# The low part of the down weights: made by Pool at the head of a turn, in place of VectorE

## The chip, the core and the metric

The kernel runs on one core of one Trainium2 chip. The metric is the time of one execution on the device in microseconds, taken as the median of several runs. TensorE (PE) multiplies matrices, VectorE (DVE), ScalarE (ACT) and Pool (GpSimd) work on tiles element by element, and SyncE (SP) issues the loads and stores.

## What is computed

One step of a two-layer decoder over 1024 prompt tokens and 8 x 8 sample tokens: layer 0 mixes tokens by latent attention, layer 1 by causal pooling, and each is followed by a gated FFN with a short causal convolution. The part that matters here is that FFN (from the reference):

```python
D_MODEL, D_FF, CONV_W = 1024, 2816, 3

def conv_ffn(h, prev, w_up, conv_w, conv_b, w_down):
    T = h.shape[1]
    u = h @ w_up
    up = jnp.concatenate([prev.astype(u.dtype), u], axis=1)
    conv = conv_b + up[:, 0:T] * conv_w[0]
    for k in range(1, CONV_W):
        conv = conv + up[:, k:k + T] * conv_w[k]
    y = (jax.nn.silu(conv[..., :D_FF]) * conv[..., D_FF:]) @ w_down
    return y, up[:, -CONV_BUF:]
```

## The kernel before

All is float32, kept with model or FFN rows on the partitions and tokens along the columns. TensorE multiplies in a shorter format, so each operand is split into a high part (ACT copies it into fp32r) and a low part (the difference), and a product is three matmuls: high x high, high x low, low x high.

The change lies in the last stage, `tail_stage`, whose FFN runs in 88 **turns** n = 0 to 87 (the code calls them pairs): two layers, in each the tokens in two halves, 22 turns to each of the four stretches. A **first half** (turns 0 to 21 and 44 to 65) has 512 columns, worked in one piece; a **second half** (turns 22 to 43 and 66 to 87) has 576, in two pieces of 288. Turn n covers 128 gate rows and the 128 up rows that go with them, and uses three weight tiles of 128 x 1024:

- G and U, the gate and the up weights of turn n. TensorE makes G, then U (`up`, lines 2742 to 2744), in 8 steps a piece.
- D, down weights. They lag: between the up steps of turn n, at places that tables fix (`DOWN_AT`), TensorE makes the down products of turn n-2 (`down`, lines 2706 to 2708), with g = silu(gate) x up of the two turns 2j and 2j+1. A D tile covers half of the model rows for both of these turns. So the first down product of an even turn n waits for g of turn n-1, and that of an odd turn finds it made.

Each tile goes the same way: SP loads it into one of two `raw` buffers, ACT makes `w_hi` (`split_hi`, L2380), and VectorE makes `w_lo` (`split_lo`, L2511), counted by the semaphore `lo_ready`. Loading, high and low parts all follow one list, `order`: U of turn n, G of turn n+1, D of turn n-1, and so on. A `raw` buffer is loaded again when the low part of its tile is done. There is one D slot: its high part waits for the last down product of the tile before, which stands near the end of a turn, so ACT makes D's high part at the very end of a turn and VectorE its low part at the head of the next.

What VectorE does in the head of turn n, in this order: D of n-2 (L2511), in a first half U of n too (L2511 again), the convolution of U of turn n-1 (L2530, L2535 for the samples), g = gate x up (L2542), then, when ACT has copied g into `g_hi` (L2435), its low part `g_lo` (L2548). Later in the turn come additions of the down products out of PSUM into `y` (L2563), the convolution of G, and the low part of the next G; in a second half U's too.

Beside it run `Chain`s, the norms and mixers of the other half of the tokens, cut into six ticks a turn that every engine goes through in program order. On Pool a chain has additions of squares (L2102), additions to the residual x (L2107), and in the pooling mixer of layer 1 window sums (L2061, L2151). Turns of a chain's quiet parts and the last 15 turns have nothing on Pool.

Every engine runs its own instructions in program order and waits at semaphores. The order within each is written out by hand.

Of the kernel before, what the change touches and what calls it, by code (L numbers as in the profile page):

```python
# [18 lines left out]
ALU = mybir.AluOpType  # L19
# [89 lines left out]
class Kernel:  # L109
# [22 lines left out]
    def sem(self, name):  # L132

        self.sems.append(self.nc.alloc_semaphore(name=name))
        return self.sems[-1]
# [1346 lines left out]
N_PAIRS = 4 * PAIRS  # L1482
SLOTS = 6
TICKS = SLOTS * PAIRS
# [4 lines left out]
G, U, D = range(3)  # L1489
# [87 lines left out]
class Tail:  # L1577


    def __init__(self, k, own):  # L1580
# [23 lines left out]
        sem = lambda name: k.sem("t_" + name)  # L1604
# [4 lines left out]
        self.hi_ready = sem("hi_ready")  # L1609
        self.lo_ready = sem("lo_ready")  # L1610
        self.o_hi_ready, self.o_lo_ready = sem("o_hi_ready"), sem("o_lo_ready")
# [572 lines left out]
def tail_stage(k):  # L2184
    nc, io = k.nc, k.io
    with ExitStack() as own:
        t = Tail(k, own)
# [3 lines left out]
        chains = []  # L2191
# [9 lines left out]
        order = [("out", j) for j in range(OUT_UNITS)] + [(G, 0)]  # L2201
# [3 lines left out]
        number = {what: o for o, what in enumerate(order)}  # L2205

        def slot(s, n):

            if s == "out":
                return (n + 1) % 3  # L2210
            return G if s == D and n == N_PAIRS - 2 else s

        def unit(s, n):
# [3 lines left out]
            return io["ffn_w"][n // PAIRS // 2, n % PAIRS, s]  # L2217

        def conv_steps(s, n):

            whole, rest = divmod(n, PAIRS)
            each = (2, 4) if s == G else (2, 6)
            return sum(each[q % 2] for q in range(whole)) * PAIRS + each[whole % 2] * rest
# [43 lines left out]
        def _(sp):  # L2267
            def load(o):
                if o >= 2:
                    sp.wait_ge(t.lo_ready, o - 1)  # L2270
                sp.dma_start(t.raw[o % 2][:], unit(*order[o])).then_inc(t.raw_in[o % 2], 16)
# [69 lines left out]
            sp.wait_ge(t.x_out, 80)  # L2341

        @block.gpsimd
        def _(pool):
            pool.memset(t.y[0][:, :, 0:BUF], 0.0).then_inc(t.zeroed, 1)
            for j in range(OUT_UNITS):
                chains[0].pool(pool, 2 * j)
                chains[0].pool(pool, 2 * j + 1)
            pool.wait_ge(t.x_in[1], 16)
            for chain in chains[1:5]:  # L2350
                for tick in range(TICKS):
                    chain.pool(pool, tick)
            for tick in range(SLOTS):
                chains[5].pool(pool, tick)
# [151 lines left out]
        def split_lo(dve, s, n):  # L2506

            o = number[s, n]
            dve.wait_ge(t.hi_ready, o + 1)
            i = slot(s, n)  # L2510
            dve.tensor_tensor(t.w_lo[i][:], t.raw[o % 2][:], t.w_hi[i][:], ALU.subtract).then_inc(t.lo_ready, 1)  # L2511
# [54 lines left out]
        def _(dve):  # L2566
# [21 lines left out]
            for n in range(N_PAIRS):  # L2588
                q, p = divmod(n, PAIRS)
# [7 lines left out]

                if n >= 2:
                    split_lo(dve, D, n - 2)
                if not half_of(n):  # L2600
# [35 lines left out]
                else:  # L2636
# [19 lines left out]
                    sums(*((3, 4) if few else (7, 8)))  # L2656
            split_lo(dve, D, N_PAIRS - 2)
            split_lo(dve, D, N_PAIRS - 1)
            convolve(dve, U, N_PAIRS - 1, 1)
# [8 lines left out]
        def _(pe):  # L2668
            def out_unit(j, c):
                half = j // KT  # L2670
                cols, bank = piece(half, c), out_bank(j, c)
                pe.wait_ge(t.lo_ready, number["out", j] + 1)
                if j >= KT + 2:
# [15 lines left out]
            def down(r):  # L2689
# [4 lines left out]
                bank = down_bank(r)[:, 0:cols.stop - cols.start]  # L2694
                pe.wait_ge(t.lo_ready, number[D, m] + 1)
                pe.wait_ge(t.g_lo_ready, before(first + 1) + c + 1)
# [26 lines left out]
            def up(s, n, c):  # L2723
# [5 lines left out]
                places = DOWN_AT[half][len(downs) > 4]  # L2729
                pe.wait_ge(t.lo_ready, number[s, n] + 1)  # L2730
                bank_free(s, n, c)
# [213 lines left out]
```

## Time and profile before

| | us |
|---|---|
| median of 3 runs (2517.59 to 2523.27) | 2517.89 |
| the profiled execution | 2525.76 |
| its span, first to last instruction | 2522.9 |
| PE busy in it | 2405.1 |
| DVE busy in it | 1678.1 |
| ACT busy in it | 1229.2 |
| POOL busy in it | 340.2 |

The profile is of one execution. Its times are in microseconds from the first instruction; busy times do not count waits at semaphores. A row of a timeline says when an instruction started, how long it took, its engine, line and tiles, and in brackets how long the engine had been idle before it and what released it. "x2" merges two neighbours that follow each other; their time is then that from the start of the first to the end of the last. An instruction's time includes what it stands and waits for inside the engine.

### The profile page before, as it was taken

How to read it: one execution, taken by the hardware profiler on the slowest of the kernel's cores; microseconds unless marked ns; L12 is line 12 of the kernel's file. 1: busy time of each engine (PE TensorE's matmuls, PEld its weight loads, DVE VectorE, ACT ScalarE, POOL GpSimd, SP SyncE). 2: the span in 40 equal slices, each digit the busy share in tenths (PEclk: the TensorE clock that was granted, in tenths of full speed). 3: DMA queues.
4: the chain of work that ended last, by engine and by line, in shares of the span. 5: the costliest groups of instructions: out<-in, count | busy, mean ns of one | idle time of the engine just before them, and what ended most of it. 6: DMA issues, size and time to landing. Idle time of an engine off the chain costs nothing.

```text
span 2522.9 us, 40509 instructions
## 1 busy us (share of the span) xinstructions
PE 2405.1 (95%) x15148; PEld 2059.6 (82%) x15148; DVE 1678.1 (67%) x2953; ACT 1229.2 (49%) x2734; POOL 340.2 (13%) x365
## 2 busy tenths in 40 slices
PE   7989999998989989999999999999999999999996
PEld 6966666766668878888899999997778889999995
DVE  5655666666234678666677858777866877766666
ACT  4444444443234655434556455555645555444443
POOL 0000000000004240000131113013222202100003
PEclk9999999999899999999999999999999999999998
DMA  7022223225534223232322222232223222232221
GB/s 274 13 93 93 97 93 116 101 102 210 191 111 163 76 76 96 89 100 92 109 84 76 76 71 81 77 116 97 91 70 100 91 93 82 93 110 78 89 80 69
DMA packets 71714, 253.50 MB, mean 100 GB/s; under 512 B 7874, under 2 KB 15426, under 8 KB 64610
## 3 DMA queue, kind: packets, MB, share of 16 engines
q1 hardware_dynamic: 71090, 250.78, 29.2%
q8 instruction: 122, 2.00, 0.3%
q14 instruction: 70, 0.57, 0.1%
q10 hardware_dynamic: 432, 0.15, 0.0%
HBM read 243.83 MB, written 7.07 MB: 99 GB/s over the span
## 4 chain that ended last, share of the span: by engine, by line
PE 61%; DVE 6%; issue 1%; ACT 1%; POOL 1%; DMA 0%; DVEq 0%; POOLq 0%; ACTq 0%
PE psum L2743 12%; PE psum L2744 12%; PE psum L2742 12%; PE psum L2706 6%; PE psum L2707 6%; PE psum L2708 6%; DVE t_conv L2530 1%; PE psum L2684 1%; PE psum L2686 1%; PE psum L2685 1%; DVE t_w_lo L2511 1%; PE psum L2178 1%; DVE t_y L2563 1%; PE psum L2163 1%; POOL t_stat L2102 1%
## 5 line engine op out<-in xcount | busy, mean ns | idle before, releaser
L2742 PE MATMUL psum<-t_h,t_w_hi 128*128 128x288 f32 (+1 forms) x2112 | 699.2, 331 | 3.4 <-DVE t_w_lo L2511 3.4
L2743 PE MATMUL psum<-t_h,t_w_hi 128*128 128x288 f32 (+1 forms) x2112 | 693.5, 328 | 0.0
L2744 PE MATMUL psum<-t_h,t_w_lo 128*128 128x288 f32 (+1 forms) x2112 | 692.8, 328 | 0.0
L2742 PEld LDWEIGHTS psum<-t_h,t_w_hi 128*128 128x128 f32 x2112 | 397.5, 188 | 36.9 <-DVE t_w_lo L2511 5.4
L2743 PEld LDWEIGHTS psum<-t_h,t_w_hi 128*128 128x128 f32 x2112 | 397.6, 188 | 31.5
L2744 PEld LDWEIGHTS psum<-t_h,t_w_lo 128*128 128x128 f32 x2112 | 398.0, 188 | 27.9
L2563 DVE TENSOR_TENSOR t_y<-psum,t_y 128x288 f32<-128x288 f32 (+1 forms) x480 | 255.1, 532 | 247.7 <-PE psum L2708 245.7
L2511 DVE TENSOR_TENSOR t_w_lo<-t_raw,t_w_hi 128x1024 fp32r<-128x1024 f32 x280 | 350.9, 1265 | 83.3 <-ACT t_w_hi L2380 83.1
L2380 ACT ACTIVATE t_w_hi<-t_raw 128x1024 fp32r<-128x1024 f32 x280 | 295.6, 1066 | 175.0 <-PE psum L2708 157.4
L2706 PE MATMUL psum<-t_g_hi,t_w_hi 128*128 128x288 f32 (+1 forms) x1056 | 348.4, 330 | 16.3 <-issue 7.2
L2530 DVE SCALAR_TENSOR_TENSOR t_conv<-t_u,t_taps,t_conv 128x512 f32<-128x512 f32 (+2 forms) x440 | 307.4, 699 | 80.1 <-ACT t_conv L2418 75.3
L2707 PE MATMUL psum<-t_g_lo,t_w_hi 128*128 128x288 f32 (+1 forms) x1056 | 346.7, 328 | 0.0
L2708 PE MATMUL psum<-t_g_hi,t_w_lo 128*128 128x288 f32 (+1 forms) x1056 | 346.4, 328 | 0.0
L2102 POOL TENSOR_TENSOR t_stat<-t_stat,t_sq 128x256 f32<-128x256 f32 (+1 forms) x196 | 185.3, 949 | 1148.8 <-ACT t_sq L1882 1141.8
L2706 PEld LDWEIGHTS psum<-t_g_hi,t_w_hi 128*128 128x128 f32 x1056 | 198.5, 188 | 37.6 <-issue 16.5
L2707 PEld LDWEIGHTS psum<-t_g_lo,t_w_hi 128*128 128x128 f32 x1056 | 198.4, 188 | 15.6
L2708 PEld LDWEIGHTS psum<-t_g_hi,t_w_lo 128*128 128x128 f32 x1056 | 198.6, 188 | 15.1
L2409 ACT ACTIVATE t_u<-psum 128x512 f32<-128x512 f32 (+2 forms) x264 | 116.8, 442 | 133.0 <-PE psum L2744 116.5
L2435 ACT ACTIVATE t_g_hi<-t_conv 128x288 fp32r<-128x288 f32 (+1 forms) x132 | 66.8, 506 | 229.7 <-DVE t_conv L2542 229.5
L2418 ACT ACTIVATE t_conv<-psum,t_taps 128x288 f32<-128x288 f32 (+1 forms) x264 | 174.3, 660 | 0.0
L1141 PE MATMUL psum<-keys,q 128*128 128x512 f32 (+3 forms) x384 | 150.8, 502 | 3.4 <-ACT prob L921 2.2
L928 ACT ACTIVATE prob_t<-psum 128x512 f32<-128x512 f32 (+3 forms) x128 | 66.1, 517 | 139.9 <-PE psum L1157 137.4
(215 smaller groups left out, 3375.3 us busy)
## 6 DMA issues: line engine op xcount, KB each, us to landing
t_raw<-in_ffn_w SPq DMA_DIRECT2D x264, 512.0 KB, 3.5
late_w<-in_ada_late SPq DMA_DIRECT2D x40, 1024.0 KB, 4.8
cache<-in_cache SPq DMA_DIRECT2D x64, 320.0 KB, 4.7
t_raw<-in_wo SPq DMA_DIRECT2D x16, 512.0 KB, 3.3
ada_w<-in_ada_w SPq DMA_DIRECT2D x6, 1024.0 KB, 8.5
proj_raw<-in_proj_w SPq DMA_DIRECT2D x8, 448.0 KB, 7.9
x<-in_pair_w SPq DMA_DIRECT2D x4, 768.0 KB, 5.3
x<-in_x SPq DMA_DIRECT2D x1, 2304.0 KB, 11.7
```

The source lines that it names most:

```text
L2102: pool.tensor_tensor(acc, acc, t.sq[:, r % 2, 0:self.T], ALU.add).then_inc(t.added, 1)
L2380: act.activation(t.w_hi[slot(s, n)][:], t.raw[o % 2][:], ACT.Copy).then_inc(t.hi_ready, 1)
L2418: act.activation(t.conv[s][:, cols], bank[:, 0:n_all], ACT.Identity, bias=t.taps[:, layer, m, 3:4], scale=t.taps[:, layer, m, 2:3]).then_i ...
L2511: dve.tensor_tensor(t.w_lo[i][:], t.raw[o % 2][:], t.w_hi[i][:], ALU.subtract).then_inc(t.lo_ready, 1)
L2530: dve.scalar_tensor_tensor(prompt, u[:, tap + first:tap + last], by, prompt, ALU.mult, ALU.add)\
L2563: dve.tensor_tensor(y, out, y, ALU.add).then_inc(t.acc_done, 1)
L2706: pe.matmul(bank, t.w_hi[i][:, o], hi, start=e == 0, stop=False)
L2707: pe.matmul(bank, t.w_hi[i][:, o], lo, start=False, stop=False)
L2708: last = pe.matmul(bank, t.w_lo[i][:, o], hi, start=False, stop=e == 1)
L2742: pe.matmul(bank, t.w_hi[s][:, o], hi, start=kt == 0, stop=False)
L2743: pe.matmul(bank, t.w_hi[s][:, o], lo, start=False, stop=False)
L2744: last = pe.matmul(bank, t.w_lo[s][:, o], hi, start=False, stop=kt == KT - 1)
```

## The change

Two methods are new. `split_down_lo` lets Pool wait for the high part of D of turn n, subtract, and count a semaphore of its own, `down_lo_ready`. `low_part` lets an engine wait for the low part of a tile: for D by that semaphore, for the others by `lo_ready`, renumbered without the D tiles. SP (before it loads a `raw` buffer again) and TensorE (`up`, `down` and the output projection) wait through it. Pool makes D of n-2 at the head of its ticks of turn n, from turn 2 on, and the last two D tiles after the last turn. The three calls on VectorE go.

```diff
-        self.lo_ready = sem("lo_ready")
+        self.lo_ready, self.down_lo_ready = sem("lo_ready"), sem("down_lo_ready")
...
+        lo_number = {what: sum(w[0] != D for w in order[:o]) for o, what in enumerate(order)}
+
+        def low_part(eng, s, n):
+
+            if s == D:
+                eng.wait_ge(t.down_lo_ready, n + 1)
+            else:
+                eng.wait_ge(t.lo_ready, lo_number[s, n] + 1)
...
-                    sp.wait_ge(t.lo_ready, o - 1)
+                    low_part(sp, *order[o - 2])
...
+        def split_down_lo(pool, n):
+
+            o = number[D, n]
+            pool.wait_ge(t.hi_ready, o + 1)
+            i = slot(D, n)
+            pool.tensor_tensor(t.w_lo[i][:], t.raw[o % 2][:], t.w_hi[i][:], ALU.subtract).then_inc(t.down_lo_ready, 1)
...
-            for chain in chains[1:5]:
+            for q, chain in enumerate(chains[1:5]):
                 for tick in range(TICKS):
+                    n, at = divmod(TICKS * q + tick, SLOTS)
+                    if at == 0 and n >= 2:
+                        split_down_lo(pool, n - 2)
                     chain.pool(pool, tick)
+            split_down_lo(pool, N_PAIRS - 2)
+            split_down_lo(pool, N_PAIRS - 1)
...
-                if n >= 2:
-                    split_lo(dve, D, n - 2)
                 if not half_of(n):
                     split_lo(dve, U, n)
...
-            split_lo(dve, D, N_PAIRS - 2)
-            split_lo(dve, D, N_PAIRS - 1)
...
-                pe.wait_ge(t.lo_ready, number[D, m] + 1)
+                low_part(pe, D, m)
```

The line numbers of the last stage are some 20 higher after the change: L2511 becomes L2532, L2530 L2551, L2542 L2563, L2548 L2569, L2563 L2584; Pool's split is L2357.

On VectorE, the head of turn 6 (a first half) before: the two splits at its start are D of turn 4 and U of turn 6, the convolution is that of U of turn 5.

```order
L2563 TENSOR_TENSOR t_y<-psum,t_y 128x512 x2
L2511 TENSOR_TENSOR t_w_lo<-t_raw,t_w_hi 128x1024 x2
L2530 SCALAR_TENSOR_TENSOR t_conv<-t_u,t_taps,t_conv 128x512 x2
L2542 TENSOR_TENSOR t_conv<-t_conv 128x512
L2548 TENSOR_TENSOR t_g_lo<-t_conv,t_g_hi 128x512
L1943 SCALAR_TENSOR_TENSOR t_scaled<-x,ada,t_stat 128x288
```

The same place after:

```order
L2584 TENSOR_TENSOR t_y<-psum,t_y 128x512 x2
L2532 TENSOR_TENSOR t_w_lo<-t_raw,t_w_hi 128x1024
L2551 SCALAR_TENSOR_TENSOR t_conv<-t_u,t_taps,t_conv 128x512 x2
L2563 TENSOR_TENSOR t_conv<-t_conv 128x512
L2569 TENSOR_TENSOR t_g_lo<-t_conv,t_g_hi 128x512
L1943 SCALAR_TENSOR_TENSOR t_scaled<-x,ada,t_stat 128x288
```

One of the two splits is gone; U's is now the first of the head, and all behind it is as it was.

On Pool, turns 25 and 26 before, where a chain squares and adds:

```order
L2107 TENSOR_TENSOR x<-x,t_y 128x256 x3
L2102 TENSOR_TENSOR t_stat<-t_stat,t_sq 128x256
L2107 TENSOR_TENSOR x<-x,t_y 128x256
L2102 TENSOR_TENSOR t_stat<-t_stat,t_sq 128x256
L2107 TENSOR_TENSOR x<-x,t_y 128x256
L2102 TENSOR_TENSOR t_stat<-t_stat,t_sq 128x256
L2107 TENSOR_TENSOR x<-x,t_y 128x256
L2102 TENSOR_TENSOR t_stat<-t_stat,t_sq 128x256 x2
```

And after:

```order
L2107 TENSOR_TENSOR x<-x,t_y 128x256 x2
L2102 TENSOR_TENSOR t_stat<-t_stat,t_sq 128x256
L2107 TENSOR_TENSOR x<-x,t_y 128x256
L2102 TENSOR_TENSOR t_stat<-t_stat,t_sq 128x256
L2107 TENSOR_TENSOR x<-x,t_y 128x256
L2102 TENSOR_TENSOR t_stat<-t_stat,t_sq 128x256
L2107 TENSOR_TENSOR x<-x,t_y 128x256
L2357 TENSOR_TENSOR t_w_lo<-t_raw,t_w_hi 128x1024
L2102 TENSOR_TENSOR t_stat<-t_stat,t_sq 128x256 x2
```

The split of turn 26 stands behind the last x addition of turn 25 and ahead of the additions of turn 26; that of turn 25 stands between the first and the second of the three x additions.

## Rows read from the trace of the kernel before

**Rows 1.** The page, part 1: busy time, share of the span, instructions.
```profile
PE 2405.1 (95%) x15148; PEld 2059.6 (82%) x15148; DVE 1678.1 (67%) x2953; ACT 1229.2 (49%) x2734; POOL 340.2 (13%) x365
```
**Rows 2.** TensorE's waits in the whole span: total us, times, longest.
```profile
PE psum L2163 <- POOL t_stat L2102: 13.3, 4, 5.4
PE psum L2706 <- issue: 7.2, 7, 1.4
...
PE psum L2706 <- DVE t_w_lo L2511: 5.6, 6, 1.6
...
PE psum L2742 <- DVE t_w_lo L2511: 3.4, 4, 1.6
PE psum L2706 <- DVE t_y L2563: 3.0, 5, 1.3
```
**Rows 3.** Groups by shape: busy us, mean ns of one, idle before it.
```profile
L2511 DVE TENSOR_TENSOR t_w_lo<-t_raw,t_w_hi 128x1024 fp32r<-128x1024 f32 x280 | 350.9, 1265 | 83.3 <-ACT t_w_hi L2380 83.1
...
L2102 POOL TENSOR_TENSOR t_stat<-t_stat,t_sq 128x288 f32<-128x288 f32 x98 | 93.3, 955 | 587.6 <-ACT t_sq L1882 583.8
...
L2061 POOL TENSOR_TENSOR t_rooms<-t_y 128x1052 f32<-128x1052 f32 x4 | 8.2, 2055 | 83.4 <-ACT t_y L1902 55.9 <-DVE t_y L2038 27.6
```
**Rows 4.** Timelines of turn 52; then line 2563: min/median/max ns, first and last start.
```profile
1803.04 2.13 POOL L2061 TENSOR_TENSOR t_rooms<-t_y 128x1052 f32<-128x1052 f32 x1 [26.10 <-ACT t_y L1902]
1803.89 2.37 DVE L2511 TENSOR_TENSOR t_w_lo<-t_raw,t_w_hi 128x1024 fp32r<-128x1024 f32 x1
...
L2563 DVE TENSOR_TENSOR t_y<-psum,t_y x480: 441/458/694, 927.5 to 2500.6; 128x288 f32<-128x288 f32 x106, 128x512 f32<-128x512 f32 x54
```
**Rows 5.** Timelines of ACT, DVE and PE in the head of turn 6.
```profile
952.45 2.01 ACT L2380 ACTIVATE t_w_hi<-t_raw 128x1024 fp32r<-128x1024 f32 x2 [5.08 <-PE psum L2708]
...
954.89 0.78 ACT L2418 ACTIVATE t_conv<-psum,t_taps 128x512 f32<-128x512 f32 x1
...
953.54 2.36 DVE L2511 TENSOR_TENSOR t_w_lo<-t_raw,t_w_hi 128x1024 fp32r<-128x1024 f32 x2 [0.46 <-ACT t_w_hi L2380]
955.82 1.53 DVE L2530 SCALAR_TENSOR_TENSOR t_conv<-t_u,t_taps,t_conv 128x512 f32<-128x512 f32 x2
...
958.78 0.69 DVE L2548 TENSOR_TENSOR t_g_lo<-t_conv,t_g_hi 128x512 fp32r<-128x512 f32 x1 [0.70 <-ACT t_g_hi L2435]
...
959.75 0.39 PE L2706 MATMUL psum<-t_g_hi,t_w_hi 128*128 128x512 f32 x1
```
**Rows 6.** The same two steps, DVE and PE, in the head of turn 64.
```profile
2036.20 0.69 DVE L2548 TENSOR_TENSOR t_g_lo<-t_conv,t_g_hi 128x512 fp32r<-128x512 f32 x1 [0.70 <-ACT t_g_hi L2435]
...
2037.17 0.39 PE L2706 MATMUL psum<-t_g_hi,t_w_hi 128*128 128x512 f32 x1
```
**Rows 7.** The same two steps in the head of turn 50.
```profile
1775.59 0.69 DVE L2548 TENSOR_TENSOR t_g_lo<-t_conv,t_g_hi 128x512 fp32r<-128x512 f32 x1 [0.70 <-ACT t_g_hi L2435]
...
1776.39 0.47 PE L2706 MATMUL psum<-t_g_hi,t_w_hi 128*128 128x512 f32 x1 [1.32 <-issue]
```
**Rows 8.** Timelines of DVE and PE in the head of turn 78, a second half.
```profile
2293.50 1.23 DVE L2511 TENSOR_TENSOR t_w_lo<-t_raw,t_w_hi 128x1024 fp32r<-128x1024 f32 x1 [0.69 <-ACT t_w_hi L2380]
...
2296.52 0.30 PE L2706 MATMUL psum<-t_g_hi,t_w_hi 128*128 128x288 f32 x1
```
**Rows 9.** Timelines of DVE, POOL and PE in the head of turn 26, a second half.
```profile
1296.36 1.22 DVE L2511 TENSOR_TENSOR t_w_lo<-t_raw,t_w_hi 128x1024 fp32r<-128x1024 f32 x1
...
1296.52 1.55 POOL L2107 TENSOR_TENSOR x<-x,t_y 128x256 f32<-128x256 f32 x1 [2.62 <-DVE t_y L1991]
...
1298.48 0.30 PE L2706 MATMUL psum<-t_g_hi,t_w_hi 128*128 128x288 f32 x1
```
**Rows 10.** Timeline of PE at the first down product of turn 31.
```profile
1398.88 0.40 PE L2706 MATMUL psum<-t_g_hi,t_w_hi 128*128 128x288 f32 x1 [0.93 <-DVE t_w_lo L2511]
```

More of the change, by code:

```diff
@@ L2671, in out_unit @@
                 cols, bank = piece(half, c), out_bank(j, c)
-                pe.wait_ge(t.lo_ready, number["out", j] + 1)
+                low_part(pe, "out", j)
                 if j >= KT + 2:
@@ L2729, in up @@
                 places = DOWN_AT[half][len(downs) > 4]
-                pe.wait_ge(t.lo_ready, number[s, n] + 1)
+                low_part(pe, s, n)
                 bank_free(s, n, c)
```

## The prediction

> **What bounds the kernel now.** I read the page first, then who waited for whom on TensorE, then the timelines around the moved step, turn by turn. The page says that TensorE (PE) is busy for 95% of the span, VectorE (DVE) for 67%, Pool for 13% [rows 1]. So work taken off VectorE is worth only what TensorE waits for it. In the 88 FFN turns those waits are few [rows 2]: 7.2 us in 7 waits in front of the first down product of a turn (L2706) that the profile puts to "issue", 5.6 us in 6 for a low part of weights, 3.0 us in 5 for an accumulation, and 3.4 us in 4 in front of an up product. Together that is 19 us of 2523: the most that a lighter VectorE could give. The 13.3 us at L2163 are for Pool's own adds.
>
> The "issue" waits are explained by a timeline. In turn 50 VectorE's subtraction for the low part of g (L2548) ends at 1775.59 + 0.69 = 1776.28, and the waiting matmul starts at 1776.39, 0.1 us later [rows 7]: TensorE waits for g_lo. This holds in every even turn of a first half (512 columns), and in turns 22 and 66 behind them, because the down products of an even turn need the g of the turn just ended, and that g is finished only in the head of the same turn: VectorE makes the low part of the down weights (D), then that of the up weights (U), then the convolution of U (L2530), the product (L2542), ACT copies it, VectorE makes g_lo, and TensorE starts L2706. I count 18 such turns from turn 4 on: in ten of them g_lo ends 0.1 us ahead of the matmul (7 of these are the "issue" waits), in eight 0.28 us ahead. The eight are 6, 10, 12, 14, 16, 20, 58 and 64; the first and the last stand in [rows 5] and [rows 6]: 958.78 + 0.69 = 959.47 against 959.75, and 2036.89 against 2037.17. Since a matmul released by g_lo starts 0.1 us after it, the true slack in these is 0.18 us. **This chain, not VectorE's share of busy time, is what the change must be priced on.**
>
> **The moved step's price.** 88 subtractions of 128x1024 leave VectorE, where one takes 1.265 us in the mean [rows 3]; back to back they follow each other every 1.14 us (two and the start of the convolution: 955.82 - 953.54 = 2.28) [rows 5]. That is 88 x 1.14 = 100 us of VectorE, nearly all of it beside TensorE work. On Pool no row has this width with this output type. The nearest is the 128x1052 addition, 2055 ns; 2055 x 1024/1052 gives 2.00 us. The far end is the 128x288 addition's 955 ns, which by columns gives 3.40 us, though it has its fixed part and its blocked cases in it [rows 3]. I take 2.05 us, by the row nearest in size; 2.0 to 3.4 stay for the range. A start on Pool after ACT's signal I set at 0.08 us, an estimate.
>
> **What Pool does to VectorE.** In turn 52 a Pool addition ran from 1803.04 to 1805.17; VectorE's split, started inside it at 1803.89, took 2.37 us instead of 1.22 and ended 1.09 us after Pool [rows 4]. So VectorE did not share, it stood until Pool was through. The accumulations of L2563, which read PSUM and one SBUF tensor, never exceeded 694 ns in 480 cases, Pool or not [rows 4]: only VectorE's instructions with two SBUF inputs stand. It goes the other way too: in turn 26 Pool's 128x256 addition started at 1296.52, while VectorE's split ran, and took 1.55 us [rows 9]. The splits, convolutions, products and g_lo all have two SBUF inputs. The Trainium skill, in "SBUF — State Buffer", section "Who interferes with whom", speaks against this change: it calls the hold an exclusive lock for the whole instruction, with whichever of the two starts second stopped until the first is through. The trace agrees (2.37 against 1.22 us); without such a lock the sum would be rival 1 below.
>
> **Turn 6, step by step** [rows 5]. ACT's two copies take 2.01 us together; the first ends at 953.51, the second at 954.46. Before: D on VectorE at 953.54, U behind it, convolution at 955.82; ACT has had its input ready since 954.89 + 0.78 = 955.67. After: Pool starts D at 953.59 and ends at 955.64. VectorE's U is ready at 954.46, but stands until Pool ends; it ends 1.09 later and the convolution starts 0.08 ahead of that end, so at 956.64: 0.82 us later than before, although an instruction has left the queue. g_lo ends at 960.29, TensorE starts at 960.39 instead of 959.75: **0.64 us lost**. TensorE makes nothing of it good, since the next turn's head starts from its own last product.
>
> **The sum.**
> - Eight such turns x 0.64 = 5.1 us.
> - Turns 8, 18 and 62, whose slack is used up (0.1 us) without a visible wait: 0.4, 0.8, 0.8 = 2.0 us.
> - Turns 22 and 66: U comes later there, and the convolution waits for ACT until 1.2 us after D's high part. Pool holds it until 2.0: 0.7 each = 1.4 us.
> - Turns 4, 48, 50, 52 and 60 have the wait already, and Pool's additions ahead of the split; the convolution comes 0.85 to 1.3 us later: 5.0 us.
> - Turn 3: TensorE waits at L2163 for additions of Pool [rows 2], and the split now stands between them; 1.0 us, from 0.5 to 1.9.
> - Second halves, ordinary turns: the first down product starts 3.02 us after D's split may start (2296.52 - 2293.50) [rows 8]. Pool's needs 0.05 to start, 2.05, and 0.06 to reach TensorE. Nothing lost; the convolution comes 0.8 us later, covered by the time that is left before U's low part is wanted half a turn later.
> - Turns 26 to 28 and 37 to 39: one of Pool's x additions is still ahead of the split in its order. In turn 26 it starts at 1296.52; with about 0.74 us for itself the split starts at 1297.3 at the earliest and ends at 1299.3, but TensorE wants it at 1298.48 [rows 9]: 0.9 us, or 1.3 if a piece of the convolution gets in between. Four such turns at 1.0, two with 0.7 us more room at 0.25: 4.5 us.
> - Turns 30, 31 and 41 to 43, where TensorE waits for D itself. In turn 31 it has been idle since 1398.88 - 0.93 = 1397.95 [rows 10], and D, which released it, began 1.22 + 0.06 us before 1398.88, at 1397.60. Pool's ends at 1399.7: 0.8 us worse. The others, where VectorE was late itself: 0.3 to 0.4 each. 2.3 us.
> - The end of turn 87, where both splits of the last pair stand in Pool and the convolution behind them: 0.8 us.
> - Turns 53 and 54, where VectorE is full: D off its queue against Pool's holds, three times 1.1 against up to 2.0; I take 0, plus or minus 3.
>
> Sum 22.1 us. The loads lose nothing: SP's load of the next G waits for D, comes 0.8 us later, and lands some microseconds before ACT wants it. The added semaphore stops Pool until D's high part is there; behind it stand that turn's additions, and behind them ACT's squares (two buffers), in turns that hold no second chain mostly none.
>
> The profiled execution took 2525.76 us (span 2522.9), 7.9 above the median of 2517.89; a difference made on its trace is put on the median: 2517.9 + 22.1 = **2540 us**. With the terms' own spread (2.0 to 2.3 us for the split on some 27 places, minus 1 to plus 7; turn 3, turns 26 to 39 and turns 53, 54, about 5 either way) 2531 to 2550.
>
> Of Pool's price the Trainium skill's "GPSIMD Engine Reference", section "Performance versus the Vector engine", gives 4497 ns for 2048 columns; half is 2.25 us as an estimate. By that the sum would be 22.1 + 27 x 0.2 = 27.5 us, 2545. The trace's 1052 columns in 2.06 us speak for less.
>
> **Rivals.**
> 1. *Side by side.* Pool's split and VectorE's U run without stopping each other. Then U starts at ACT's second signal, the waits that hang on VectorE's queue go (7.2 of "issue" less 2.8 in turns 22 and 66, 3.4 and 3.0 [rows 2]: 10.8 us), and D comes 0.9 us later where TensorE waits for it (1.5 us): 9 us faster, 2509. It decides for faster as soon as the hold costs under 0.2 us. Against it: the 2.37 us of [rows 4]. Chance 8%.
> 2. *A slow Pool.* The fp32r output or the subtraction goes at the 955 ns row's rate, 3.4 us. Then every place above costs 1.35 more (36 us), and in the second halves D lands 3.5 us after the signal against 3.05: 0.5 us in some 34 turns. 22 + 36 + 17 = 75 us, 2593. For it: no row of Pool writes fp32r. Against it: on VectorE the type costs nothing, 1.22 us for 1024 columns. Chance 15%, anywhere from 2550 up.
> 3. *A draw.* The stops in the clean turns are real (8 us with turns 8, 18, 22, 62 and 66), but in the busy turns 4 and 48 to 60 VectorE gains 1.14 us a turn and Pool's hold falls onto accumulations that read PSUM and are not stopped; the gains there take back 5 of the 8: about 2521. For it: L2563 stands among the heads' steps. Chance 15%.
>
> The forecast has 62%. A measurement of this kernel can tell about 0.3% (7.6 us) from no change: slower is the forecast and rival 2, 77%; within it is rival 3 with a part of rival 1, 18%; faster 5%. The range 2517 to 2556 leaves out rival 1 and most of rival 2.
>
> **What will show it.** Pool's split at 1.9 to 2.3 us; VectorE's U beginning in first-half heads before Pool ends and lasting up to 2.2 us instead of 1.22; a wait of 0.5 to 0.8 us in front of L2706 in even turns of first halves, put to "issue" or to g_lo; L2706 waiting for Pool in turns 26 to 39; no new waits in turns 73 to 87. I am wrong if U is not stretched (rival 1), if Pool's split is over 2.9 us (rival 2), or if the waits appear and the total does not.

## The result and the profile after

The changed kernel took 2571.81 us, the median of 3 runs (2571.66 to 2573.66), against 2517.89: a ratio of 1.0212, 95% interval [1.0192, 1.0232]. In a later job (runs measured together), with four runs of it and seven of the kernel before, it was 2568.64 against 2522.78: 1.0186 [1.0166, 1.0205]. So the change costs 46 to 54 us. The direction was forecast, the size was not: 22 us were.

The page of the changed kernel, part 1, answers to [rows 1]:

```profile
PE 2417.4 (94%) x15148; PEld 2065.0 (80%) x15148; DVE 1688.6 (66%) x2865; ACT 1230.2 (48%) x2734; POOL 549.7 (21%) x453
```

VectorE has 88 instructions less and is busy 10 us longer. Where that comes from, the groups by shape show (busy us, mean ns of one; see [rows 3]):

```profile
L2532 DVE TENSOR_TENSOR t_w_lo<-t_raw,t_w_hi 128x1024 fp32r<-128x1024 f32 x192 | 283.6, 1478 | 106.4 <-ACT t_w_hi L2401 106.4
...
L2551 DVE SCALAR_TENSOR_TENSOR t_conv<-t_u,t_taps,t_conv 128x512 f32<-128x512 f32 x264 | 223.9, 848 | 67.0 <-ACT t_conv L2439 63.3
```
```profile
L2357 POOL TENSOR_TENSOR t_w_lo<-t_raw,t_w_hi 128x1024 fp32r<-128x1024 f32 x88 | 217.1, 2468 | 796.8 <-ACT t_w_hi L2401 796.6
```

The remaining splits on VectorE take 1478 ns in the mean instead of 1265: they stand. Pool's split takes 2468 ns, where the prediction took 2.05 us. TensorE's waits in the whole span (total us, times, longest), beside [rows 2]:

```profile
PE psum L2723 <- issue: 27.5, 20, 3.0
PE psum L2723 <- POOL t_w_lo L2357: 14.8, 12, 2.1
PE psum L2163 <- POOL t_stat L2102: 14.7, 5, 6.4
...
PE psum L2759 <- DVE t_w_lo L2532: 5.4, 4, 2.1
PE psum L2723 <- DVE t_y L2584: 5.4, 6, 1.8
```

L2723 is the first down product (L2706 before). Its waits put to "issue" (that is, to g_lo) grew from 7.2 us in 7 to 27.5 in 20, and those for D from 5.6 in 6 to 14.8 in 12.

**Turn 6**, against [rows 5], ACT, POOL, DVE, DVE, DVE and PE:

```profile
953.02 2.01 ACT L2401 ACTIVATE t_w_hi<-t_raw 128x1024 fp32r<-128x1024 f32 x2 [4.86 <-PE psum L2725]
...
954.16 2.41 POOL L2357 TENSOR_TENSOR t_w_lo<-t_raw,t_w_hi 128x1024 fp32r<-128x1024 f32 x1 [4.84 <-ACT t_w_hi L2401]
...
955.06 2.59 DVE L2532 TENSOR_TENSOR t_w_lo<-t_raw,t_w_hi 128x1024 fp32r<-128x1024 f32 x1 [1.41 <-ACT t_w_hi L2401]
957.57 1.53 DVE L2551 SCALAR_TENSOR_TENSOR t_conv<-t_u,t_taps,t_conv 128x512 f32<-128x512 f32 x2
...
960.52 0.69 DVE L2569 TENSOR_TENSOR t_g_lo<-t_conv,t_g_hi 128x512 fp32r<-128x512 f32 x1 [0.70 <-ACT t_g_hi L2456]
...
961.31 0.47 PE L2723 MATMUL psum<-t_g_hi,t_w_hi 128*128 128x512 f32 x1 [0.83 <-issue]
```

Pool's split starts 0.08 us after ACT's signal and ends at 956.57. VectorE's U starts 0.90 us into it, is shown with 2.59 us, and ends at 957.65, 1.08 after Pool: its own work begins when Pool is through. All behind it follows, and TensorE idles.

**Turn by turn.** The time from one turn's first up product to the next one's (for turn 87, to TensorE's last product), after minus before, sums to 50.4 us over the 88 turns. 35.4 us of it are longer waits of TensorE (one in front of a turn's first up product counts with the turn before), 15.0 us are products that run slower or start again behind a wait. Behind TensorE's last product the changed kernel gains 0.8 us, and ahead of turn 0, where nothing changed, its profile is 2.7 us shorter. By the terms of the prediction's sum:

| turns | forecast | turns longer by | of it TensorE's waits |
|---|---|---|---|
| 6, 10, 12, 14, 16, 20, 58, 64 | 5.1 | 9.2 | 7.1 |
| 8, 18, 62 | 2.0 | 3.6 | 3.2 |
| 22, 66 | 1.4 | 4.9 | 2.0 |
| 4, 48, 50, 52, 60 | 5.0 | 13.2 | 7.7 |
| 3 | 1.0 | 0.5 | 1.0 |
| 26 to 28, 37 to 39 | 4.5 | 7.7 | 6.2 |
| 30, 31, 41 to 43 | 2.3 | 5.3 | 5.0 |
| 53, 54 | 0 | 1.4 | 0.5 |
| turn 87 and behind it | 0.8 | 1.1 | 1.3 |
| 5, 45, 46, 55, 56, 61 | not named | 2.6 | 1.4 |
| all others | 0 | 0 | 0 |

Every place that was named lost, and hardly any other did. What was wrong is the size of nearly every term.

### The profile page after: what moved, and what is told of

It reads as the page before. It is cut to its first block, busy times and chain, and to the rows that moved or that the text cites. A ratio compares the mean times of both kernels' runs of the same rounds, so it can differ in the third digit from the quotient of the medians.

```text
span 2569.8 us, 40509 instructions
## 1 busy us (share of the span) xinstructions
PE 2417.4 (94%) x15148; PEld 2065.0 (80%) x15148; DVE 1688.6 (66%) x2865; ACT 1230.2 (48%) x2734; POOL 549.7 (21%) x453
## 4 chain that ended last, share of the span: by engine, by line
PE 54%; DVE 8%; issue 3%; ACT 3%; POOL 2%; DMA 1%; ACTq 0%; DVEq 0%; POOLq 0%
PE psum L2759 11%; PE psum L2760 11%; PE psum L2761 11%; PE psum L2723 6%; PE psum L2725 6%; PE psum L2724 6%; DVE t_conv L2551 3%; DVE t_w_lo L2532 2%; PE psum L2701 1%; PE psum L2703 1%; PE psum L2702 1%; PE psum L2178 1%; POOL t_stat L2102 1%; DVE t_y L2584 1%; ACT t_w_hi L2401 1%
## 5 line engine op out<-in xcount | busy, mean ns | idle before, releaser
L2551 DVE SCALAR_TENSOR_TENSOR t_conv<-t_u,t_taps,t_conv 128x512 f32<-128x512 f32 (+2 forms) x440 | 369.6, 840 | 143.2 <-ACT t_conv L2439 137.9
L2723 PE MATMUL psum<-t_g_hi,t_w_hi 128*128 128x288 f32 (+1 forms) x1056 | 352.2, 334 | 47.8 <-issue 27.5
L2584 DVE TENSOR_TENSOR t_y<-psum,t_y 128x288 f32<-128x288 f32 (+1 forms) x480 | 254.8, 532 | 209.5 <-PE psum L2725 208.3
L2357 POOL TENSOR_TENSOR t_w_lo<-t_raw,t_w_hi 128x1024 fp32r<-128x1024 f32 x88 | 217.1, 2468 | 796.8 <-ACT t_w_hi L2401 796.6
L2532 DVE TENSOR_TENSOR t_w_lo<-t_raw,t_w_hi 128x1024 fp32r<-128x1024 f32 x192 | 283.6, 1478 | 106.4 <-ACT t_w_hi L2401 106.4
L2725 PE MATMUL psum<-t_g_hi,t_w_lo 128*128 128x288 f32 (+1 forms) x1056 | 348.4, 330 | 0.0
L2723 PEld LDWEIGHTS psum<-t_g_hi,t_w_hi 128*128 128x128 f32 x1056 | 199.6, 189 | 74.3 <-issue 42.8
L2102 POOL TENSOR_TENSOR t_stat<-t_stat,t_sq 128x256 f32<-128x256 f32 (+1 forms) x196 | 189.9, 973 | 285.6 <-ACT t_sq L1882 278.5
L2725 PEld LDWEIGHTS psum<-t_g_hi,t_w_lo 128*128 128x128 f32 x1056 | 199.9, 189 | 15.7
```

What stands on the lines that cost most here:

```text
L2102: pool.tensor_tensor(acc, acc, t.sq[:, r % 2, 0:self.T], ALU.add).then_inc(t.added, 1)
L2357: pool.tensor_tensor(t.w_lo[i][:], t.raw[o % 2][:], t.w_hi[i][:], ALU.subtract).then_inc(t.down_lo_ready, 1)
L2551: dve.scalar_tensor_tensor(prompt, u[:, tap + first:tap + last], by, prompt, ALU.mult, ALU.add)\
L2584: dve.tensor_tensor(y, out, y, ALU.add).then_inc(t.acc_done, 1)
L2723: pe.matmul(bank, t.w_hi[i][:, o], hi, start=e == 0, stop=False)
L2725: last = pe.matmul(bank, t.w_lo[i][:, o], hi, start=False, stop=e == 1)
```

## Experiments

**1. Is it the bookkeeping?** VectorE makes D again, at the old place, on the new semaphore.

```diff
...
-                        split_down_lo(pool, n - 2)
...
+                if n >= 2:
+                    split_down_lo(dve, n - 2)
                 if not half_of(n):
                     split_lo(dve, U, n)
...
```

> The low part of D is made by VectorE again, at its old place, but counted on its own semaphore, and SyncE and TensorE wait through the new rule. Chain theory (Pool's split holds VectorE's head of a turn, or lands too late): nothing is left to cost, 2518 us, within 5 us of the kernel before. Rival, the bookkeeping (own semaphore, renumbered waits, the order in which SyncE sees the two raw buffers free): it carries a good part of the 54 us, 2530 to 2572 us.

Measured: 2521.39 us, ratio 0.9994 [0.9982, 1.0005]; the turns differ from those of the kernel before by 0.3 us in sum. The semaphore, the renumbered waits and SyncE's order cost nothing.

**2. Is it the length of Pool's split?** Half of its columns.

```diff
-            pool.tensor_tensor(t.w_lo[i][:], t.raw[o % 2][:], t.w_hi[i][:], ALU.subtract).then_inc(t.down_lo_ready, 1)
+            some = slice(0, D_MODEL // 2)
+            pool.tensor_tensor(t.w_lo[i][:, some], t.raw[o % 2][:, some], t.w_hi[i][:, some], ALU.subtract).then_inc(t.down_lo_ready, 1)
```

> Pool makes only the first 512 of the 1024 columns of D's low part; the low part of the other half is left out of the computation. Everything else is as in the changed kernel. Chain theory: the split takes about 1.27 us instead of 2.41, ends before VectorE's U would have been through, and the 0.83 us waits of the even first-half turns go altogether; what stays is a rest in turns 28, 39, 48 to 60: 2521 to 2530 us. Rival, price by duration: half of the 54 us stays, about 2545. Rival, the place (one more engine in the chain, whatever it does there): 2555 us or more.

Measured: 2521.71 us, ratio 0.9993 [0.9983, 1.0003]. Half the length takes away not half of the loss but all of it. Turn 6 of this run, POOL and DVE:

```profile
947.90 1.29 POOL L2358 TENSOR_TENSOR t_w_lo<-t_raw,t_w_hi 128x512 fp32r<-128x512 f32 x1 [4.84 <-ACT t_w_hi L2402]
```
```profile
948.81 1.48 DVE L2533 TENSOR_TENSOR t_w_lo<-t_raw,t_w_hi 128x1024 fp32r<-128x1024 f32 x1 [1.41 <-ACT t_w_hi L2402]
950.21 1.53 DVE L2552 SCALAR_TENSOR_TENSOR t_conv<-t_u,t_taps,t_conv 128x512 f32<-128x512 f32 x2
```

U stands for 0.4 us only, and the convolution starts 2.39 us after D's high part (947.82) against 2.31 before: the 0.18 us of slack cover that. So the loss of the whole kernel is what Pool's split lasts beyond some 1.3 us. Turn by turn it is not nothing everywhere: 28, 30, 39 and 52 still lose 0.6 to 0.8 us each, and 41 to 43, 53 and 87, where TensorE had waited for VectorE before, gain about as much.

**3 and 4. Which turns carry it?** Pool makes D in the even turns of the first halves and turns 22 and 66 only, or in all others only. These are 23 and 65 splits by the traces, not the 24 and 64 that the expectations count. A rule decides for each D tile, and the counts of the two semaphores follow it.

```diff
+        pool_turn = lambda n: n < N_PAIRS and n % 2 == 0 and (not half_of(n) or n % PAIRS == 0)
...
-                    if at == 0 and n >= 2:
+                    if at == 0 and n >= 2 and pool_turn(n):
...
+                if n >= 2 and not pool_turn(n):
+                    split_lo(dve, D, n - 2)
```

> Pool makes D only in the even turns of the first halves and in turns 22 and 66 (24 of 88 splits); the others are on VectorE. Chain theory: by the turns of the changed kernel's trace these carry 11.5 + 15.8 + 4.9 = 32 us, so 2550 us (2545 to 2556). Rival, each split costs the same wherever it stands: 24/88 of 54 us = 15 us, 2533 us.

> The complement: Pool makes D in the odd turns of the first halves, in the second halves but for turns 22 and 66, and at the end (64 of 88 splits). Chain theory: 18 us by the same turns, nearly all in turns 26 to 43 and at the end, 2536 us (2532 to 2543). Rival, each split costs the same: 39 us, 2557 us.

Measured: 2547.45 us, 1.0100 [1.0081, 1.0118], and 2547.37 us, 1.0104 [1.0086, 1.0121], against 2521.95. The first is inside its forecast by time, at 25.5 us less than the 32 expected; the second costs 25.4 us, 7 more than expected. 23 splits cost as much as the other 65, so the count is not what is paid for; but the halves stand otherwise than I read them from one trace. TensorE's waits add up: 17.7 us more than before in the one, 18.6 in the other, together 36.3 for the changed kernel's 35.4. They do not all stand where the expectations put them: the even turns and 22 and 66 hold 20.8 us of the changed kernel's waits, of which experiment 3 has 17.6, and experiment 4, where VectorE makes D in these turns, still has 3.6 (in turns 8, 10, 48, 50, 52, 60 and 64). So a part of what an even turn loses hangs on Pool's splits in other turns. The rest of the difference is what follows the waits. Turn 22, TensorE's busy time and its granted clock (PEclk) in four stretches of the changed kernel, and the second and third of them in experiment 3:

```profile
1227.30:1233.30 6.00, 4.89 (x37) 4.65 (x35) 3.91 (x4) 3.36 (x6) 2.41 (x1) 1.00 0.18 48
1233.30:1236.30 3.00, 1.68 (x6) 1.38 (x7) 1.83 (x2) 1.58 (x5) 0.00 (x0) 0.92 0.22 85
1236.30:1239.30 3.00, 3.00 (x14) 2.96 (x13) 0.69 (x1) 0.00 (x0) 0.00 (x0) 0.51 0.57 172
1239.30:1244.00 4.70, 4.70 (x30) 4.25 (x29) 3.45 (x6) 3.04 (x8) 0.00 (x0) 1.00 0.00 2
```
```profile
1232.80:1235.80 3.00, 1.64 (x8) 1.39 (x9) 1.83 (x2) 1.62 (x5) 0.00 (x0) 1.00 0.23 90
1235.80:1238.80 3.00, 3.00 (x21) 2.78 (x21) 0.93 (x2) 1.36 (x6) 0.00 (x0) 1.00 0.48 172
```

The columns are the stretch, its length, then busy time (and instructions) of PE, PEld, DVE, ACT and POOL, PEclk, DMA share and GB/s. TensorE idled 2.43 us in the one and 2.44 in the other. In the changed kernel the clock stood at 0.51, the 1.2 GHz level, for the next 3 us (14 products instead of 21), and the turn lost 1.55 us on top of its wait; in experiment 3 it stayed at full speed and nothing was lost. So it is in turn 66 (2.42 us in both), and in turn 48 (2.44 and 2.12). Experiment 4 in turn drew a drop, as such a stretch at the lower clock is called from here on, in turn 31 (1.5 us) that the changed kernel's profile does not have, behind the same wait of 2.1 us.

**5. The changed kernel again**, to see which drops belong to it.

> The changed kernel once more, beside more runs of the kernel before. If the clock drops behind long waits of TensorE come and go from run to run, the profile has the same waits (35 us more than before in the FFN turns) but drops in other turns; if they belong to the kernel, the same six turns (4, 22, 48, 52, 53, 66) show them. Ratio 1.018 to 1.022.

Measured: ratio 1.0186. The waits are the same to 0.2 us in sum (35.2 more than before); turns 4, 22, 52 and 66 show the drop again, 48 and 53 do not. So the waits belong to the kernel, the drops behind them in part to the run: 9.0 us in the six turns 4, 22, 48, 52, 53 and 66 in the first profile, 5.8 in the second, which has one in turn 87 instead. The kernel before has such waits too: at the same 3.3 us of wait, turn 1 is 1.0 to 2.6 us shorter than in its profile in six of the later ones.

**6. Do the long waits cost the clock?** TensorE fills them, with products that are thrown away.

```diff
+                if m + 2 in (4, 22, 48, 52, 66) and r == 4 * before(m):
+                    half = half_of(m + 2)
+                    some = piece(half, 0)
+                    few = t.h[half][:, 0, 0, some]
+                    pe.wait_ge(t.acc_done, r - 1)
+                    for _ in range(15 if half else 9):
+                        pe.matmul(down_bank(r)[:, 0:some.stop], t.w_hi[G if half else U][:, 0:P], few, start=True, stop=True)
                 low_part(pe, D, m)
```

> The changed kernel, and in turns 4, 22, 48, 52 and 66 TensorE fills some 2.0 us of the wait in front of the first down product with matmuls whose result is thrown away (9 of 512 columns, 15 of 288 in turns 22 and 66). The waits' end is set by VectorE and stays. Clock theory: the idle of over 2 us was what the clock dropped for; with it filled the drops in these turns (1.3 + 1.5 + 1.4 + 1.9 + 1.3 = 7.4 us) go: 5 to 8 us below the changed kernel in the same job. Rival, the slower running behind the wait is something else, such as the work that has piled up on VectorE: no difference, within 2 us of it.

Measured: 2564.26 us, 4.4 below the changed kernel in the same job where 5 to 8 were expected, 1.0172 [1.0152, 1.0192]. Turn by turn the five are shorter by 1.57, 1.55, 1.38, 1.69 and 1.33 us than in its first profile, 7.5 together, though the down product starts no earlier (7.36 us into turn 22 against 7.35); against the second profile, which lacked the drop of turn 48, it is 5.7. In turn 22 the granted clock is now 1.00 throughout:

```profile
1223.50:1229.50 6.00, 6.00 (x47) 6.00 (x46) 3.91 (x4) 3.34 (x6) 2.40 (x1) 1.00 0.17 63
1229.50:1232.50 3.00, 2.54 (x15) 2.07 (x14) 1.83 (x2) 1.61 (x5) 0.00 (x0) 1.00 0.14 55
1232.50:1235.50 3.00, 3.00 (x21) 2.78 (x21) 0.95 (x2) 1.39 (x6) 0.00 (x0) 1.00 0.50 175
```

The drops are the idle's and not a backlog of VectorE's, whose queue is as long as before.

**7. Does g_lo set the even turns?** The four down products of an even first-half turn stand later.

```diff
-DOWN_AT = (((10, 11, 13, 15), (4, 5, 6, 7, 10, 11, 13, 14)), ((11, 16, 21, 26), (8, 11, 14, 17, 20, 23, 26, 29)))
+DOWN_AT = (((12, 13, 14, 15), (4, 5, 6, 7, 10, 11, 13, 14)), ((11, 16, 21, 26), (8, 11, 14, 17, 20, 23, 26, 29)))
```

> The changed kernel with the four down products of an even first-half turn behind up steps 12, 13, 14, 15 instead of 10, 11, 13, 15, so that the first wants g two steps (1.38 us) later. Chain theory (g_lo is late by 0.83 us in clean turns, by 1.1 to 2 in busy ones): the waits of the 12 or so clean even turns go (1.08 each, 13 us), and 1.0 to 1.4 us in each of turns 4, 48, 50, 52, 60: 17 to 21 us below the changed kernel, 2550 to 2555 us, unless the sums at the end of the turn now wait. Rival, TensorE waits there for something else than g (D itself, U's low part): 5 us or less.

> The same table in the kernel before. Chain theory: only waits that are there can go, those of turns 4, 48, 50, 52, 60 (0.45 to 1.3 us each): 3 to 5 us faster than the kernel before, ratio 0.998 to 0.999. Rival, the sums pile up at the end of the turn: slower by 3 us or more.

Measured: 2575.22 us (1.0215) and, in the kernel before, 2541.76 us (1.0076 [1.0053, 1.0099]). Both totals miss; in the kernel before the rival, sums that pile up, has the right sign. The turns tell why: against the changed kernel 6, 8, 10, 12, 14, 16, 18, 20, 58, 62 and 64 are shorter as expected, by 0.85 to 1.35 us each and 11.8 together, of which 9.6 are waits. Turns 4, 48 and 60 are 1.4 to 1.9 us shorter, though only 0.3, 0.5 and 1.3 us of their waits go. But turn 5 is 5.8 us longer and turns 54 to 56 11.7, and in the kernel before 3.9 and 14.0. Most of that in turns 54 to 56 stands at L2178, a product of the other half's chain, whose waits for ACT go from 2.2 us in 2 to 10.1 in 3:

```profile
PE psum L2178 <- ACT t_y L1924: 10.1, 3, 4.2
...
PE psum L2723 <- issue: 8.8, 5, 2.4
```

That the sums, which now crowd at the turn's end, push the chain's steps back on VectorE is argued from the order, not traced. Later products would cure the wait for any late input; that it is g_lo in the clean even turns is read from turn 6 of the changed kernel, where D was through at 956.57, U at 957.65 and g_lo at 961.21, 0.10 us ahead of the product. The "issue" waits in front of L2723 fall from 27.5 us in 20 to 8.8 in 5, but this table is no cure.

**8. What does Pool's split cost, and why?** Other forms of it, in turns where Pool has nothing else.

```diff
+            if n in (75, 76):
+                done = pool.tensor_tensor(t.scratch[:], raw[:], hi[:], ALU.subtract)
+            elif n in (77, 78):
+                done = pool.tensor_tensor(lo[:], raw[:], hi[:], ALU.add)
...
+            elif n in (81, 82):
+                done = pool.tensor_tensor(lo[:], raw[:], raw[:], ALU.add)
...
+            elif n in (9, 11):
+                done = pool.tensor_tensor(t.scratch[:, 0:1020], raw[:, 4:], raw[:, 0:1020], ALU.add)
```

> A price list of Pool's split in turns where Pool has nothing else. Turns 75, 76: subtraction into an f32 tile of its own; 77, 78: addition into the fp32r tile; 79, 80: addition into the f32 tile; 81, 82: addition of raw to itself, fp32r; 83, 84: the same, f32; 85, 86: subtraction of 512 columns; 9, 11: addition of raw to raw shifted by 4 columns, f32, 1020 columns; 13, 15: the same as four rows of 255, shifted by one; 17, 19: addition into one of its own inputs. In these turns D's low part is left out or replaced by a sum. If the type written makes the difference, the f32 turns take about 2.05 us and the fp32r ones 2.40; if the operation, the additions take 2.05; if that both inputs come from one tensor, the turns 81 to 84 and 9 to 15 take 2.05 and 75 to 80 take 2.40; if neither, all take 2.40 but those of 512 columns (1.28) and the 2.05 us additions were cheap for another reason.

The groups by shape (x2 each; the mean is the number before the second bar):

```profile
L2362 POOL TENSOR_TENSOR t_w_lo<-t_raw,t_w_hi 128x1024 fp32r<-128x1024 f32 x2 | 4.8, 2406 | 33.4 <-ACT t_w_hi L2424 33.4
L2360 POOL TENSOR_TENSOR t_scratch<-t_raw,t_w_hi 128x1024 f32<-128x1024 f32 x2 | 4.8, 2404 | 33.4 <-ACT t_w_hi L2424 33.4
L2364 POOL TENSOR_TENSOR t_scratch<-t_raw,t_w_hi 128x1024 f32<-128x1024 f32 x2 | 4.8, 2400 | 33.4 <-ACT t_w_hi L2424 33.4
...
L2366 POOL TENSOR_TENSOR t_w_lo<-t_raw 128x1024 fp32r<-128x1024 f32 x2 | 3.8, 1894 | 33.9 <-ACT t_w_hi L2424 33.9
L2368 POOL TENSOR_TENSOR t_scratch<-t_raw 128x1024 f32<-128x1024 f32 x2 | 3.8, 1894 | 34.4 <-ACT t_w_hi L2424 34.4
L2372 POOL TENSOR_TENSOR t_scratch<-t_raw 128x1020 f32<-128x1020 f32 x2 | 3.8, 1887 | 30.5 <-ACT t_w_hi L2424 30.5
```

Neither the type written (2406 against 2400 ns for the addition) nor the operation (2404 against 2400 in f32) matters. Two inputs from two tensors take 2.40 us, two from one tensor 1.89, also when they are shifted against each other. The row that the prediction scaled, L2061, reads one tensor twice. The kernel's own split, with nothing beside it in turn 2, takes 2.37.

**9. The whole kernel at the lower price.** Pool adds raw to itself in all 88 places.

```diff
-            pool.tensor_tensor(t.w_lo[i][:], t.raw[o % 2][:], t.w_hi[i][:], ALU.subtract).then_inc(t.down_lo_ready, 1)
+            pool.tensor_tensor(t.w_lo[i][:], t.raw[o % 2][:], t.raw[o % 2][:], ALU.add).then_inc(t.down_lo_ready, 1)
```

> The changed kernel, but Pool adds raw to itself (the form that took 1.89 us in the price list) where it subtracted; D's low part is replaced by that sum, all else stays. If the prediction's sum was right but for the price of the split, the whole kernel at 1.89 us loses 22.1 - 27 x 0.16 = 18 us against the kernel before: ratio 1.007. If the sum also left out what a wait costs beyond its idle time (0.25 us behind each new one, and slower running behind those over 2 us), then by the changed kernel's turns: 35 us of waits less some 31 places x 0.51 = 16, so 19 us of waits, and 4 to 8 us behind them: 23 to 27 us, ratio 1.009 to 1.011. If the price of the split is not what the loss hangs on: 1.018 or more.

Measured: 2541.90 us, 1.0083 [1.0063, 1.0103], 20.7 us above the kernel before in its job. 0.51 us less per split take 25 us off (45.9 less 20.7; 24 to 27 by the turns of the two profiles). TensorE's waits:

```profile
PE psum L2723 <- issue: 15.9, 18, 2.1
...
PE psum L2723 <- POOL t_w_lo L2357: 9.0, 10, 1.6
```

Turn 6 loses 0.57 us instead of 1.08. The waits are 16.5 us above those before (19 expected), what runs slower behind them 6.6. The time lies between the two forecasts, and the interval holds part of both; by the turns, the price is the main thing and the rest is there as well.

**10. Pool's split ahead of the open x addition** in turns 26 to 28 and 37 to 39.

```diff
-                    if at == 0 and n >= 2:
+                    if at == 0 and n >= 2 and n not in (26, 27, 28, 37, 38, 39):
                         split_down_lo(pool, n - 2)
+                    if at == 5 and n + 1 in (26, 27, 28, 37, 38, 39):
+                        split_down_lo(pool, n - 1)
```

> In turns 26 to 28 and 37 to 39 Pool's split stands ahead of its last tick of the turn before, so ahead of the x addition that was still open there. Chain theory: the split then starts 0.08 us after D's high part instead of 0.98 to 1.08, the waits of these six turns (0.94, 0.47, 1.70 and the like, 7.7 us with the restarts) go or shrink to a third, unless the addition that now stands behind the split is wanted: 5 to 8 us below the changed kernel (2568.6 to 2571.8). Rival, the split itself is too slow whatever stands ahead of it, or VectorE holds it: less than 2 us.

Measured: 2568.76 us, no different from the changed kernel (1.0189 [1.0172, 1.0206]); 5 to 8 us were expected. In its profile these six turns are 3.9 us shorter, half of the 7.7 that they had lost; a drop behind turn 31's wait took 1.5 back. In turn 26 the split now starts 0.08 us after D's high part and lasts 2.50 us, and TensorE does not wait for it. Over the span, the waits of the first down product's line (L2725 here) for D and for VectorE's sums are, against 14.8 in 12 and 5.4 in 6 of the changed kernel:

```profile
PE psum L2725 <- POOL t_w_lo L2357: 8.9, 8, 2.1
...
PE psum L2725 <- DVE t_y L2586: 7.4, 9, 1.8
```

In the six turns the waits for D fall from 6.2 us to 0.4 (in turns 28 and 39). What still is lost there stands mostly at later down products of the same turns, which come late for VectorE's sums: in turn 26 0.5 us at 14.29 us into the turn, with a wait of 0.32. VectorE's convolution in the head of that turn had been held by the split:

```profile
1312.37 1.81 DVE L2553 SCALAR_TENSOR_TENSOR t_conv<-t_u,t_taps,t_conv 128x224 f32<-128x224 f32 x1 [0.71 <-ACT t_conv L2441]
```

It took 0.83 us in the kernel before. So the addition ahead of the split carried the waits for D; with those gone, the hold on VectorE shows behind them, at half the price. That the sums are late because of it is argued from their order on VectorE.

**11. The split in two instructions** of 512 columns.

```diff
-            pool.tensor_tensor(t.w_lo[i][:], t.raw[o % 2][:], t.w_hi[i][:], ALU.subtract).then_inc(t.down_lo_ready, 1)
+            for some in (slice(0, D_MODEL // 2), slice(D_MODEL // 2, D_MODEL)):
+                done = pool.tensor_tensor(t.w_lo[i][:, some], t.raw[o % 2][:, some], t.w_hi[i][:, some], ALU.subtract)
+            done.then_inc(t.down_lo_ready, 1)
```

> Pool makes the same split in two instructions of 512 columns. Hold theory, one stands until the other engine's instruction is through, and the one that waits goes next: VectorE's U ends 2.43 us after D's high part as in the run with half the columns, then Pool's second half holds the convolution until about 3.6: the clean even turns lose about as much as in the changed kernel or a little more (1.1 to 1.3 us). If Pool keeps the right of way between its two instructions, U and all behind it come as in the changed kernel, 0.1 to 0.2 us later: 1.2 us a turn. If the engines share instead of standing, the two instructions change nothing. 2568 to 2580 us; the second halves lose up to 0.2 us more where D is late.

Measured: 2573.95 us, 1.0205 [1.0182, 1.0228], as the changed kernel. Turn 6, POOL (both halves in one row), then DVE:

```profile
954.48 3.54 POOL L2358 TENSOR_TENSOR t_w_lo<-t_raw,t_w_hi 128x512 fp32r<-128x512 f32 x2 [4.82 <-ACT t_w_hi L2403]
```
```profile
955.38 1.48 DVE L2534 TENSOR_TENSOR t_w_lo<-t_raw,t_w_hi 128x1024 fp32r<-128x1024 f32 x1 [1.41 <-ACT t_w_hi L2403]
956.77 2.57 DVE L2553 SCALAR_TENSOR_TENSOR t_conv<-t_u,t_taps,t_conv 128x512 f32<-128x512 f32 x2
```

The engines take turns: Pool's first half, VectorE's U (through at 956.86), Pool's second half, stretched from 1.29 to 2.28 us and through at 958.02, and only then the convolution, which takes 2.57 us instead of 1.53. What is not paid in front of U is paid behind it.

## Why the prediction was right in direction and wrong in size

**What bounds the kernel, and the hold: right.** The loss hangs on g_lo in even first-half turns, as 27.5 us in 20 "issue" waits show, and on D in turns 26 to 43. VectorE's instructions with two SBUF inputs stand until Pool is through, and the other way round (experiments 2 and 11); the accumulations, which read PSUM and one SBUF tensor, again never exceeded 694 ns in 480 cases. The Trainium skill's "SBUF — State Buffer", section "Who interferes with whom", says that the order of issue decides who blocks; the alternation in experiment 11 agrees. Rival 1 (side by side) fell with the 2.59 us of U, rival 3 (a draw) with turns 4 and 48 to 60, which lost most of all.

**The moved step's price: the step that failed.** I chose between 2.0 and 3.4 us by the row nearest in size, and took 2.05. It was 2.41. The row nearest in kind would have been one with two different tensors as inputs, such as L2102 [rows 3]. From experiments 2 and 8 such an instruction takes (2.41 - 1.29)/512 = 2.19 ns a column and some 0.17 us besides, so 0.80 us for 288 columns; half of that row's 98 take 0.81 us or less, the 955 ns of its mean have the held cases in them, and 3.40 by columns multiplied the fixed part with them. The trace of the kernel before had two rows of the right kind that the prediction did not use, multiplications of two different tensors on Pool:

```profile
L1088 POOL TENSOR_TENSOR rope_rows<-rope_rows,rot 128x384 f32<-128x384 f32 x8 | 8.1, 1008 | 444.7 <-DVE rope_by_sin L982 444.7
...
L1088 POOL TENSOR_TENSOR rope_rows<-rope_rows,rot 128x320 f32<-128x320 f32 x4 | 3.5, 878 | 23.2 <-DVE rope_by_sin L982 23.2
```

They give (1008 - 878)/64 = 2.03 ns a column, and 1008 + 640 x 2.03 = 2307 ns for 1024 columns, an estimate 0.1 us below what was measured. The range was narrowed as well: 2.0 to 3.4 us had been kept for it, but 2531 to 2550 was worked out with 2.0 to 2.3. The Trainium skill's "GPSIMD Engine Reference", section "Performance versus the Vector engine", has the rate itself, some 2.6 cycles an element at 1.2 GHz for two inputs, 2.17 ns a column as an estimate, and the trace agrees (2.19). The prediction halved the page's time for 2048 columns instead and got 2.25.

In turn 6 this is the whole error but 0.08 us. The down product was forecast 0.64 us late; 0.36 us more of Pool make it 1.00, and its row says the same: the product ahead of it starts at 960.08, the next is due 0.23 us later, at 960.31, and starts at 961.31. The wait is shown as 0.83 because that product is drawn 0.39 us long. Behind the wait the first product takes 0.08 us more (0.47), which makes the 1.08.

**The sum: mis-sized twice more.** First, I counted some 27 places at which a longer split would be paid; 39 turns lost more than 0.1 us, and experiment 9 gives 25 us for 0.51 us, 49 places' worth with what follows the waits. In turns 4 and 48 Pool's split is itself held by VectorE (2.84 and 3.40 us); in 50 and 52 it takes 2.38 and 2.42 us, but Pool's next instruction holds VectorE right behind it; in 60 additions ahead of it start it 2.0 us after D's high part. Together that is 7.7 us of waits for 5.0 forecast. Second, "TensorE makes nothing of it good" was too kind: it loses more than it waits. Behind idle times of 2 to 3 us the granted clock went to 0.5 in turns 4, 22, 48, 52, 53 and 66, 9.0 us that no term held. For turns 22 and 66 that and the price are the error: 1.0 us of wait each against 0.7 forecast, and 1.5 and 1.3 behind it.

**The second halves: right.** In turn 78 the split takes the time from 2339.31 to 2341.72, TensorE wants D at 2342.29 and does not wait, as in all ordinary second-half turns and in 73 to 86:

```profile
2339.31 2.41 POOL L2357 TENSOR_TENSOR t_w_lo<-t_raw,t_w_hi 128x1024 fp32r<-128x1024 f32 x1 [16.71 <-ACT t_w_hi L2401]
```
```profile
2342.29 0.30 PE L2723 MATMUL psum<-t_g_hi,t_w_hi 128*128 128x288 f32 x1
```

In turns 26 to 28 and 37 to 39 the place was right too: the split starts behind the x addition, and TensorE waits for it. Turn 26, POOL, then PE, against [rows 9]:

```profile
1308.78 0.64 POOL L2107 TENSOR_TENSOR x<-x,t_y 128x256 f32<-128x256 f32 x1 [2.62 <-DVE t_y L1991]
1309.37 2.38 POOL L2357 TENSOR_TENSOR t_w_lo<-t_raw,t_w_hi 128x1024 fp32r<-128x1024 f32 x1
```
```profile
1311.81 0.40 PE L2723 MATMUL psum<-t_g_hi,t_w_hi 128*128 128x288 f32 x1 [0.94 <-POOL t_w_lo L2357]
```

**Rival 2, a slow Pool**, had the right sign of the error and the wrong reason and size: the type written costs nothing, and at 2.41 us the second halves still lose nothing.

**The starting point.** The forecast was put on a median of 3 runs, 2517.89. Over the later jobs the kernel before has medians of 2521 to 2523. Some 4 of the 54 us of the first comparison are that.

No version tried beats the kernel before. In none of the 88 turns of the changed kernel did VectorE's shorter queue save TensorE anything that could be told apart. What stays open is why a clock drop follows one wait and not another of the same length, and why two different input tensors cost Pool a quarter more than one.

## What to carry to other kernels

While Pool works, moving an element-wise step to it frees VectorE only for what does not read two SBUF tensors; in a chain of such steps the move costs the difference of the two durations at every place where the chain has no slack. Take the price of the moved instruction from a row with the same kind of operands, and not only of the same size; here 0.36 us of error in it came out as some 18 us, an estimate (0.36/0.51 of the 25, some of the drops included). A wait of TensorE can cost more than its length: read the granted clock behind waits like it.

## What the runs showed that was not expected

- Pool's two-input operation: 2.40 us for 1024 columns from two tensors, 1.89 from one read twice, 1.29 for 512 from two; type and operation without effect.
- Two instructions of Pool back to back do not keep the hold: VectorE's waiting instruction goes in between (experiment 11).
- The granted clock fell to 0.51 behind a wait of 2.43 us in turn 22 and stayed at 1.00 behind one of 2.44 in another run; in experiment 9 it fell behind a wait of 1.92 us in turn 66, and did not behind the same wait in turn 22. In the first profile of the changed kernel each fall cost 1.0 to 2.4 us.
